# A hybrid decoder layer with product-key experts: the second half of the tokens placed as strands

## What is computed

```
xn  = rmsnorm(x, norm1_w)
z, xbc, dt, q, k, v, g, g_lr, merge = split(xn @ w_in)         # 1024 -> all inputs
xbc = silu(conv4(xbc) + conv_b)                                # x, B, C of the SSD
y   = ssd(x, dt, B, C) (chunks of 128) * silu(z), rms per group of 512, @ w_ssd_out
o   = rms(gla(q, k, v, gate) (chunks of 64)) * silu(g), @ w_gla_out
x   = x + (sigmoid(merge_1) * y + sigmoid(merge_2) * o) @ w_out
hn  = rmsnorm(x, norm2_w)
# PEER: 8 heads; 16 best of 128 keys twice, 16 best of the 256 sums, softmax -> gate, idx
hid = gelu(expert_u[idx] . hn);   x = x + sum(gate * hid * expert_v[idx])
out = rmsnorm(x, final_norm_w), and the SSD, convolution and GLA states
```

## Time and profile before

| | |
|---|---|
| runs, us | 2611.31, 2610.52, 3598.17 (median 2611.31) |
| profiled execution, us | 2614.99 |
| its span, us | 2612.9 |
| granted clock, mean | 0.904 |
| busy: PE, DVE, ACT, POOL | 82%, 60%, 28%, 27% |
| gathers of expert rows | 528, 545.29 MB |

### The profile page before, as it was taken

The page is one execution under the profiler, slowest core; times in us unless marked ns, Lnnn a source line. Parts: engine busy times, 40 slices in busy tenths (PEclk is TensorE's granted clock), DMA queues, the critical chain, the costliest instruction groups (busy, mean ns, idle before and its releaser), DMA issues.

```text
span 2612.9 us, 24483 instructions
## 1 busy us (share of the span) xinstructions
PE 2130.9 (82%) x7972; PEld 1348.2 (52%) x7988; DVE 1577.6 (60%) x3578; ACT 739.6 (28%) x1761; POOL 702.5 (27%) x636
## 2 busy tenths in 40 slices
PE   5888798699996967776788888997779877787786
PEld 5655365488964645553565666773525433333332
DVE  2556323233213539896666577887866777777764
ACT  2333111232102225443322333222223222222221
POOL 0212122000000222221233232333324444444452
PEclk8999799798998988888898998998879999989899
DMA  5143222442544978886788897999989999999997
GB/s 206 78 157 147 89 99 77 158 146 87 159 157 148 392 281 302 300 301 221 290 312 342 326 388 289 422 424 425 407 243 414 427 427 427 427 427 427 427 426 296
DMA packets 146402, 751.20 MB, mean 288 GB/s; under 512 B 20025, under 2 KB 39033, under 8 KB 77538
## 3 DMA queue, kind: packets, MB, share of 16 engines
q0 software_dynamic: 75008, 545.29, 52.3%
q1 hardware_dynamic: 71266, 204.33, 21.7%
HBM read 718.43 MB, written 31.07 MB: 287 GB/s over the span
## 4 chain that ended last, share of the span: by engine, by line
PE 41%; DVE 18%; DMA 14%; issue 4%; ACT 4%; POOL 1%; SPq 0%; DVEq 0%; POOLq 0%; ACTq 0%
PE bank L2467 12%; DMA t_rows<-in_experts,t_idx 12%; PE bank L2174 10%; PE bank L2404 6%; DVE t_rows L2117 6%; PE bank L2416 3%; DVE t_fin L2136 2%; PE bank L2176 2%; PE bank L2177 2%; PE bank L2178 2%; POOL t_rows L1684 1%; DMA t_hn_cur<-in_norm_f 1%; PE bank L2372 1%; DVE t_junk L1940 1%; DVE t_junk L1936 1%
## 5 line engine op out<-in xcount | busy, mean ns | idle before, releaser
L1684 POOL DMA_INDIRECT t_rows<-in_experts,t_idx x528 | 616.0, 1167 | 1511.9 <-PE bank L2467 662.9
L2467 PE MATMUL bank<-t_rows,t_diag 128*128 128x512 f32 (+1 forms) x1552 | 769.4, 642 | 194.6 <-ACT t_diag L1887 194.2
L2117 DVE CUSTOM_DVE_ANT_0 t_rows<-t_rows,t_hn_cur 128x1024 f32<-128x1024 f32 (+1 forms) x528 | 634.1, 1223 | 167.6 <-DMA t_rows<-in_experts,t_idx 167.3
L2467 PEld LDWEIGHTS bank<-t_rows,t_diag 128*128 128x128 f32 (+1 forms) x1552 | 296.7, 200 | 594.9 <-issue 335.8
L2174 PE MATMUL bank<-t_xs,t_wring 128*128 128x256 f32 (+1 forms) x1664 | 408.9, 403 | 46.6 <-ACT t_last L1712 23.2
L2174 PEld LDWEIGHTS bank<-t_xs,t_wring 128*128 128x128 f32 x1664 | 332.7, 203 | 133.3 <-issue 80.1
L1874 ACT ACTIVATE t_gel<-t_hid 128x2 f32<-128x2 f32 (+1 forms) x264 | 53.7, 203 | 638.2 <-DVE t_hid L2117 638.0
L1887 ACT ACTIVATE t_diag<-ident,t_gg 128x128 f32<-128x128 f32 x372 | 133.5, 395 | 189.5 <-DVE t_gg L2124 188.9
L2136 DVE SCALAR_TENSOR_TENSOR t_fin<-t_rows,t_gg,t_fin 128x1024 f32<-128x1024 f32 x140 | 179.9, 1285 | 7.8
L2404 PE MATMUL bank<-t_yoT,t_wring 128*128 128x264 f32 (+1 forms) x768 | 175.2, 386 | 4.2 <-DVE t_yoT L2076 4.2
L2404 PEld LDWEIGHTS bank<-t_yoT,t_wring 128*128 128x128 f32 x768 | 146.3, 192 | 34.2 <-issue 12.7
(11 more groups left out here) (388 smaller groups left out, 2436.0 us busy)
## 6 DMA issues: line engine op xcount, KB each, us to landing
t_wring<-in_w_merge SPq DMA_DIRECT2D x80, 512.0 KB, 4.8
t_wring<-in_w_z SPq DMA_DIRECT2D x32, 512.0 KB, 5.8
t_wring<-in_w_query SPq DMA_DIRECT2D x32, 512.0 KB, 7.9
ring<-in_w_ssd SPq DMA_DIRECT2D x4, 3072.0 KB, 13.2
t_wring<-in_w_ssd SPq DMA_DIRECT2D x24, 512.0 KB, 6.5
t_rows<-in_experts,t_idx POOLq DMA_INDIRECT x528, 14.3
s_sst<-in_state_ssd SPq DMA_DIRECT2D x4, 2048.0 KB, 9.3
o_sssd<-s_sst SPq DMA_DIRECT2D x16, 512.0 KB, 2.6
```

The costliest lines, as they stand in the source:

```text
L1684: nc.gpsimd.indirect_dma_start(rows[0:m, n % RING, :], None, k.dram["experts"], bass.IndirectOffsetOnAxis(idx[0:m, u, s:s + 1], 0)).then_i ...
L2117: last = nc.vector.tensor_tensor_reduce(out=v, in0=v, in1=hn_cur[0:m, r % 2, :], scale=1.0, scalar=0.0, op0=ALU.mult, op1=ALU.add, accum_o ...
L2467: last = nc.tensor.matmul(ps[bank][0:round_rows(r), :], diag[0:m, d % DIAGS, 0:round_rows(r)], rows[0:m, n % RING, D + half * 512:D + half ...
```

## The change

The order of the second half is made anew. `second_half` gives it as some sixty strands, each a list of steps in order; a step names the tasks that it comes after, a cost and its own tasks. `run_place` goes over all strands at each place (now two to a pair, each counted alone, as far as place 228) and takes every step whose predecessors were placed at least one place before (two, for TensorE's tasks), as long as PE's cost keeps within a goal and within 6 us a place. The rest of the first half is taken at 5 us a place ahead of it. The two dots of a pair are tasks of their own, and `gg`, `diag`, `acc` of a pair move behind the first dot of the next. `slot_engines` chooses for each slot PE or VectorE, by the load that the placed tasks put on either.

SiLU of the convolution becomes tanh on ACT and a product on VectorE, with the convolution's weights halved; the sigmoids of the merge become tanh with the factor one half taken into the residual addition. The second half's z and g gates are computed with tokens on partitions (`zt`: activations stationary, 512 columns moving), multiplied there (`gt`), and turned and scaled by the norm in one product with a diagonal (`dg`, `tq`, `ev`). GLA's projection is split in query and key (`gq`) and value (`gv`), its state products (`csp`) come ahead of the outputs (`go`), its state has one buffer with five steps, and its gate (`glr` to `gkd`) moves ahead of SSD. The merge's gates alternate between two pairs of banks.

```diff
+def second_half():
+
+    strands = []
+
...
+    def step(after, cost, *tasks):
+        return ([t for t in after if t], cost, list(tasks))
...
+    strand(*[x for i, (g, r) in enumerate(triples) for x in (
+        step([last_tile("cvt", prev(triples, i))], 3.5, ("su", g, r, 0)), step([], 3.5, ("su", g, r, 1)))])
+    strand(*[step([("su", g, r, 1), last_tile("sil", prev(triples, i))], 0, *two("cvt", g, r)) for i, (g, r) in enumerate(triples)])
+    strand(*[step([last_tile("cvt", t)], 0, *two("tap", *t)) for t in triples])
...
+    strand(*[step([("sil", g, CT - 1), of("ups", prev(chunks, i))], 1.5, ("xt", g, c), ("bt", g, c)) for i, (g, c) in enumerate(chunks)])
+    strand(*[step([("bt", g, c), of("yd", prev(chunks, i)), of("mxm", prev(chunks, i), 1)], 0, ("btc", g, c), ("xd", g, c)) for i, (g, c) in enumerate(chunks)])
+    strand(*[step([of("upd", prev(chunks, i)) or ("gkd",), of("dec", prev(chunks, i), 1)], 2.5, ("seg", g, c, 0), ("seg", g, c, 1)) for i, (g, c) in enumerate(chunks)])
+    strand(*[step([("seg", g, c, 1), of("yd", prev(chunks, i))], 0, ("dec", g, c, 0), ("dec", g, c, 1)) for i, (g, c) in enumerate(chunks)])
+    strand(*[step([("xd", g, c), of("ups", prev(chunks, i)), ("stl", g)], 1.8, ("yo", g, c), ("cs", g, c)) for i, (g, c) in enumerate(chunks)])
...
+    strand(*[step([("mxm", g, c, 1), ("xd", g, c), of("upd", prev(chunks, i))], 2., ("yd", g, c)) for i, (g, c) in enumerate(chunks)])
+    strand(*[step([("yd", g, c), ("yof", g, c)], 0, ("upd", g, c), ("ys", g, c), *([("sts", g)] if c else [])) for g, c in chunks])
...
+    strand(*[step([("atm", h - 1) if h else done, ("gkd",)], .5, ("cum", h)) for h in heads])
...
+    strand(*[step([("qke", h), ("goc", h - 1) if h else None], 1., ("kta", h)) for h in heads])
+    strand(*[step([("kta", h), ("go", h - 1) if h else None], 0, ("ktc", h), ("atm", h)) for h in heads])
+    strand(*[step([("ktc", h), ("vc", h)], 1.2, ("csp", h)) for h in heads])
+    strand(*[step([("csp", h), ("gsl", h)], 0, ("gst", h), ("gss", h)) for h in heads])
+    strand(*[step([("gst", h), ("atm", h)], 2.6, ("go", h), *([("gsl", h + 1)] if h + 1 < GH else [])) for h in heads])
+    strand(*[step([("go", h)], 0, ("goc", h), *([("gos", h // 2)] if h % 2 else [])) for h in heads])
...
+    strand(*[x for s in slabs for x in (
+        step([("gt", s - 2, 1) if s >= 2 else (("qk", GH - 1) if s == 0 else ("gst", GH - 1))], 3.7, ("zt", s, 0)), *[step([], 3.7, ("zt", s, u)) for u in range(1, 4)])])
+    strand(*[step([("zt", s, 3), ("sqz", s - 1) if s else done, ("gt", s - 1, 1) if s else None], 0, ("th", s, 0), ("th", s, 1)) for s in slabs])
...
+    strand(*[step([("dg", s), ("gt", s, 1), ("ev", s - 1) if s else None], 2., ("tq", s)) for s in slabs])
...
+    strand(*gates(0), *[x for j in range(KD) for x in (gates(j + 1) if j + 1 < KD else []) + merged(j)])
+    strand(*[step([("mg", 1, j, 1), ("mix", 1, j - 1) if j else ("sqz", 5)], 0, ("sig", 1, j)) for j in range(KD)])
+    strand(*[step([("sig", 1, j), ("mo", 1, j)], 0, ("mix", 1, j)) for j in range(KD)])
...
+    strand(*[x for h in range(EH) for x in (
+        step([("hs", 1, 0), ("hs", 1, 1), ("qc", 1, h - 2) if h >= 2 else None], 3.6, ("qu", 1, h, 0)), step([], 3.6, ("qu", 1, h, 1)))])
+    strand(*[step([("sco", 1, h - 2)] if h >= 2 else [("hn", 1, 1)], 0, ("kload", 1, h)) for h in range(EH)])
+    strand(*[step([("qu", 1, h, 1), ("sco", 1, h - 1) if h else None], 0, ("qc", 1, h)) for h in range(EH)])
+    strand(*[step([("qc", 1, h), ("kload", 1, h), ("sc", 1, h - 1) if h else None], 1., ("sco", 1, h)) for h in range(EH)])
+    strand(*[step([("sco", 1, h), ("ch", EH + h, 3)], 0, ("sc", 1, h)) for h in range(EH)])
...
+    def weigh_pair(u, g):
+        for kind in ("gg", "diag", "acc"):
+            order.append((kind, u, g))
...
-            order.append(("dot", u, g))
+            order.append(("dot", u, g, 0))
+            if prev is not None:
+                weigh_pair(*prev)
+            order.append(("dot", u, g, 1))
             order.append(("gelu", u, g))
+            order.append(("front", u, g, 0))
             if prev is not None:
                 finish_pair(*prev)
             if g in parts and u + 2 < len(UNITS):
                 choice_part(u + 2, parts[g])
-            order.append(("front", u, g, 0))
-            order.append(("gg", u, g))
-            order.append(("diag", u, g))
-            order.append(("acc", u, g))
             order.append(("front", u, g, 1))
             prev = (u, g)
+    weigh_pair(*prev)
...
+TENSOR_KINDS = UNIT_KINDS + ("glr", "gkp", "xt", "bt", "seg", "yo", "cs", "yd", "cum", "kta", "csp", "go", "tq", "ht", "sco")
+TENSOR_LAG, OTHER_LAG = 2, 1
+PLACE_COST = 6.
+LAST_PLACE = 2 * 114
+VECTOR_COST = {"tap": 1.45, "sil": .5, "xd": 2.05, "mxm": .7, "yof": 2.1, "ups": .7, "upd": .7, "qke": 1.3, "atm": .45, "gst": 1.95, "gt": 1.4,
+               "dg": 1., "mix": 1.3, "x1": .7, "hn": 1.6, "hms": .2, "bnd": .15, "gkd": 1.4, "gz": 1., "fadd": 1.4, "fin": 1.6, "dot": 1.3, "gg": .16}
+CHOICE_COST = (2., 2., 2.6, 2.4)
+ROW_COST = {"tensor": 1.94, "vector": 1.29}
+PAIR_TIME = 5.5
...
+    def run_place(goal):
+        nonlocal spent, place
+        place += 1
...
+        for i, steps in enumerate(strands):
+            while heads_at[i] < len(steps):
+                after, cost, tasks = steps[heads_at[i]]
+                lag = TENSOR_LAG if tasks[0][0] in TENSOR_KINDS else OTHER_LAG
+                if any(t not in place_of or place_of[t] + lag > place for t in after):
+                    break
+                if cost and (spent + cost / 2 > goal or here and here + cost > PLACE_COST):
+                    break
+                spent += cost
+                here += cost
+                for n, task in enumerate(tasks):
+                    emit(task, cost / len(tasks))
+                heads_at[i] += 1
 
     def until(task):
+        stuck = 0
         while task not in emitted:
-            take()
+            if at < len(front):
+                take()
+            else:
+                before = len(order)
+                run_place(1e9)
...
+def slot_engines(tensor_load, vector_load):
+
+    late = {"tensor": 0., "vector": 0.}
+    out = []
+    for u, (r, h) in enumerate(UNITS):
+        ends = {next(v for v, (q, _) in enumerate(UNITS) if q == r) * TOPK, (max(v for v, (q, _) in enumerate(UNITS) if q == r) + 1) * TOPK - 1}
+        for g in range(PAIRS):
+            pair = u * PAIRS + g
+            if pair:
+                late["tensor"] = max(0., late["tensor"] - PAIR_TIME) + tensor_load.get(pair, 0.)
+                late["vector"] = max(0., late["vector"] - PAIR_TIME) + vector_load.get(pair, 0.)
+            for s in range(2 * g, 2 * g + 2):
+                pick = "tensor" if late["tensor"] + ROW_COST["tensor"] <= late["vector"] + ROW_COST["vector"] else "vector"
+                if u * TOPK + s in ends or ROUNDS[r][0] == "s" or (h == 0 and g < 2):
+                    pick = "tensor"
+                late[pick] += ROW_COST[pick]
+                out.append(pick)
+    return out
...
                 elif kind == "slu":
...
-                        act.wait_ge(yo_done, 2 * (g - 1))
-                    nc.scalar.activation(xc[:, g % 2, j, :], cv[:, j % 2, :], ACT.Silu).then_inc(slu_done, 1)
+                    nc.scalar.activation(raw[:, j % 2, HIST:HIST + BT], cv[:, j % 2, :], ACT.Tanh).then_inc(slu_done, 1)
                 elif kind == "btc":
...
+                elif kind == "th":
...
+                            act.wait_ge(y_kept[i], 16 * GROUPS)
+                    nc.scalar.activation(gz[:, c, :], ps[2 + 2 * (s % 2) + c][:, :], ACT.Tanh, scale=.5).then_inc(th_done, 1)
+                elif kind == "sqz":
...
-                    nc.scalar.activation(sig[:, i, 0:width(p)], ps[G0 + i][:, 0:width(p)], ACT.Sigmoid).then_inc(sig_done, 1)
+                        act.wait_ge(tq_done, 6)
+                    for i in range(2):
+                        last = nc.scalar.activation(sig[:, i, 0:width(p)], ps[gate_bank(p, j) + i][:, 0:width(p)], ACT.Tanh, scale=.5)
+                    last.then_inc(sig_done, 1)
                 elif kind == "hsq":
...
+                elif kind == "sil":
+                    g, j = at
+                    dve.wait_ge(slu_done, g * CT + j + 1)
+                    if g >= 2:
+                        dve.wait_ge(yd_done, 2 * (g - 1))
+                        dve.wait_ge(yo_done, 2 * (g - 1))
+                    nc.vector.scalar_tensor_tensor(xc[:, g % 2, j, :], raw[:, j % 2, HIST:HIST + BT], 1.0, cv[:, j % 2, :], ALU.add, ALU.mult).then_inc(sil_done, 1)
                 elif kind == "xd":
...
+                elif kind == "gt":
+                    s, c = at
+                    z = ps[2 + 2 * (s % 2) + c]
+                    dve.wait_ge(th_done, 2 * s + c + 1)
+                    k.vlink(dve, nc.vector.scalar_tensor_tensor(gz[:, c, :], gz[:, c, :], 1.0, z[:, :], ALU.add, ALU.mult))
...
```

(64 more changed lines are left out.)

688 lines of the change are left out of this document (397 added, 291 removed).

## The result

The changed kernel takes 2540.16 us (median of four runs, 2534.87 to 2552.99) against 2611.56 before: a ratio of 0.9724, 95% interval 0.9702 to 0.9746. It is faster by 71 us where 111 were forecast. The profiled execution took 2544.91 us, its span 2542.8 at a clock of 0.920. So 2500 was 40 us too low, and the time lies inside the range.

The account below looks back on a forecast made before the run. Front bound by engines waiting for one another, rows behind it by gathers; DMA 573 + 201 + 15 = 789, about 790/0.88 = 898 us, gain 111: span 2612.9 - 111 = 2502, forecast 2500 us, range 2420 to 2615.

Parts of the forecast that it names:

- The front: Stretch from 845 us to the last query: 230 rows instead of 315, bound about 790 us, forecast length 898 us.
- The excess: Front time beyond its rows at 2.49 us each: 325 us forecast against 436, a gain of 111 us.
- the rows behind the front: Rows-only stretch after the second half's work: 2.49 us a row, bound by gathers, taken as unchanged.
- The loss term: Front: lags of half a pair to a pair absorb engines' waits, raising efficiency from 0.82 to 0.88; 790/0.88 = 898 us.
- The weighing behind the next dot: Each pair: two slots come free about 2.5 us later, priced at nothing; GELU gets a whole dot (1.2 us).
- Lockstep stays: Rival, front: VectorE, ACT and PE stay tied once a pair, efficiency 0.82, gain 46 us, 2565 us; chance 0.18.
- planner: Rival: chain falls behind, twenty units forced out without rows beside them, 72 us, total 2572 us; chance 0.06.
- The better case: Rival, front: strands run like the merge at 0.95, gain 177 us, total 2434 us; chance 0.12.
- No loss at all: Limit of the better case: front without any efficiency loss, total 2395 us; no chance of its own.
- Table loads: Rival: ACT reloads tables between GELU and tanh, exp or roots, two a pair, 295 us; 2766 at 90% exposed; chance 0.09.
- The product with a diagonal: PE, second half's gates: 48 products replace 48 transposes, 0.31 us each, 14.8 us; transposes 0.21 us each.
- The signs: Last query at row 220 to 240, 1720 to 1780 us; front DMA 370 GB/s; SSD/GLA clock over 0.93; t_fin waits halved.

Follow-up runs that it names:

- the packing: Samples' rows gathered in 8 full gathers of 128 rows instead of 16 of 64: kernel before 2588.23 us (0.9903), changed kernel 2503.12 us (0.9577).
- the control: Changed kernel with the sample unit's diagonal 128 columns wide instead of 8, still 64 partitions: 2551.35 us, 0.9753.

## Why the prediction was right, and where it was off

*The front.* Its terms came out close. 238 rows for 230. PE's other work 796.6 - 193.3 = 603 us for 598, its 99 rows 1.95 us each for 1.89. VectorE's other work 746.1 - 289.6 - 176.0 = 280 us, under the bound of 340; 137 rows there for 131. DMA moved 374 x 918/421 = 815 us' worth for 789. By the forecast's own measure, (593 + 201 + 15)/918 = 0.88, the efficiency taken. The excess was 325 us, as forecast. That it agrees to the digit is luck: 0.88 was picked between 0.82 and 0.95 and not worked out.

*The step that failed* is the rows behind the front, taken as unchanged at 2.49 us each: 77 more of them should have added 192 us there, and 234 came. The bound looked at slots of the later weighing; two other things came. First, the sample unit. The prediction's 315 rows hold sixteen half-filled slots, counted like full ones at 40 us, and at half the rate they need these 40. If full slots run at 2.49 us, the packing says what the unit really took: 20 + 25 = 45 us before, 5 over its price, and 20 + 37 = 57 us in the changed kernel, 17 over it. The idle DMA time, 6 and 18 us, says the same. So some 12 of the 40 us that are missing are the unit's, which now stands behind the front with PE alone and at 1.2 GHz; by the profiled executions, where packing gained 24 and 44 us, it is 20. The intervals of the two gains overlap, so this share is likely, not shown. Second, the rows-only rate itself, 419 GB/s where it was 427, an estimated 8 to 14 us. It shows in every run of the changed kernel and its variants (415 to 421 from 2120 to 2460 us) and in neither run of the kernel before (427 in both). Weighing in the own pair doesn't bring it back (421); its cause stays open, as do the 6 to 20 us that are then left.

*Why the front gained.* The loss term rested on waits that fit into lags. That is shown: without lags the gain is gone. That dealing by load counts is shown too, at 30 us. Both exceed the gain together, since the strands in their order without lags are worse than the order written by hand.

*The weighing behind the next dot* was counted in the front's favour (GELU has a dot's time) and at nothing for later slots. If anything it costs.

*The rivals.* "Lockstep stays" (2565) and "planner" (2572) fall with the front's 0.88 and its end at row 238. The better case (0.95) was reached in the merge and the outputs alone; SSD has VectorE 89% and PE 90% busy in 335 GB/s, so there the engines are nearly full. "No loss at all" comes to 2392 by the prediction's own terms, not 2395. "Table loads" fell at its premise: I had tanh apart from GELU. In the front the loads went down, from 133 records to 76, and SiLU's 24 calls of tanh needed one:

```profile
L1804 ACT ACT_TABLE_LOAD  x1: 1283/1283/1283, 957.8 to 957.8; - x1
```

The Trainium skill (ScalarE: Activation LUTs, Table sets) lists tanh with exp and with sigmoid, GELU in a set of its own; here the measurement decides, and the two follow each other without a load. The run with SiLU and sigmoid bounds the matter: 116 loads in place of 76, 51 us of ACT, and no measurable time.

*Prices.* The product with a diagonal cost 0.26 us (12.5 us for 48) where 0.31 was taken, still over the 0.21 of a transpose, which agrees with the Trainium skill's rule (Perfetto Trace Analysis, Transposes). At 2 us in all the price decides nothing.

*The signs.* Last query at row 238 and 1763 us, clock 0.95 and 0.96 in SSD and GLA, 137 rows on VectorE, full DMA behind 1900 us: right. DMA at 370 GB/s in SSD (335) and t_fin's waits halved (175 of 240): wrong. Of the signs against the forecast one came true, the span between rows behind the front (2.69 us where it was 2.56, both to the end), and it names the step that failed. GELU's waits grew from 139 to 158 us, but not per row.

## What to carry to other kernels

When work ends earlier, ask what ran beside it: here a half-filled unit was left alone, and filling its gathers was worth 37 us. A gather of 64 rows took as long as one of 128, so a floor counted in gathers hides what half-filled ones cost; count bytes beside it. And look again at the rate of the stretch that is taken as unchanged. In a static order for in-order queues, half a pair to a pair between a step and its user was worth some 90 us, most of it by one place for ACT's and VectorE's steps; and a load dealt by stage 30, at a nearly unchanged total.

## What was not expected of the hardware

PE stayed at 1.2 GHz while it was busy without a gap for 55 us, as long as its products took 64 partitions, with 8 columns and with 128 alike. Products over 128 partitions ran at 2.4 GHz, with 128 columns and, in the packed kernel, with 8:

```profile
1823.23 8.66 PE L2681 MATMUL bank<-t_rows,t_diag 128*8 128x512 f32 x16 [8.80 <-ACT t_diag L2019]
1832.41 3.60 PE L2681 MATMUL bank<-t_rows,t_diag 128*8 128x512 f32 x8 [0.52 <-ACT t_diag L2019]
```

3.60 us for eight records is 0.45 each, against 0.856. The Trainium skill (TensorE: Matmul & The Clock Gate, What's actually happening) has the clock follow how busy PE is; by that the 55 us should not have stayed slow, and the measurement decides. Beside other products of 128 partitions, those of 64 ran fast (28.8 us for 64 records, with the sample round second).

Gathers of 64 rows ran at half the rate of those of 128, 200 and 203 GB/s against 421, with the DMA engines busy throughout (1.02 and 1.01). So the half-filled unit costs DMA time whatever the clock, and its ten slots don't hold half as much DMA time, as the theory of the packed run had it, but about as much. Why the DMA engines stand idle for part of the unit isn't settled. The clock is likely one cause (6 us idle with 128 x 128 products, 13 with the control's 64 x 128); no run varied the ring.
